# A two-block transformer on one core: the steps of the recurrence, the rotation and the branch products laid out anew

## What is computed

```python
h = rms_norm(x, norm1_g[l])
z = h @ w_in[l]                                  # 1024 -> 8704 columns
zq, zf, zi, zg, zatt, za, zb = split(z)          # q, forget gate, v, output gate, attention, two gates
# recurrence over time, 4 heads of 128, "HgRN2"
log_f = logaddexp(log(lb), log1p(-lb) + log_sigmoid(zf)); k = -expm1(log_f)
S_t = diag(f_t) S_{t-1} + k_t v_t^T;   o_t = S_t^T q_t
o_hg = rms_norm(o_hg, hg_norm_g[l]) * sigmoid(zg)
# attention, 3 groups x 4 heads of 128, windows with dilation 1, 4, 16
qg, kg = partial_rope(qg), partial_rope(kg)      # rotates the first 32 of 128 dims: r1*c - r2*s, r2*c + r1*s
o_att = sum over groups of softmax(lse) * attention(qg, kg, vg)
y = sigmoid(za) * (o_hg @ w_branch_a[l]) + sigmoid(zb) * (o_att @ w_branch_b[l])
x = x + y @ w_out[l]
x = x + square(relu(rms_norm(x, norm2_g[l]) @ w_up[l])) @ w_down[l]
```

## Time and profile before

| | |
|---|---|
| median of 3 runs | 2459.70 us (2459.69 to 2459.79) |
| the profiled execution | 2458.67 us, its span 2457.0 us |
| granted clock of TensorE, mean | 0.955 |
| PE busy | 2200.3 us (90%) |
| DVE busy | 1641.8 us (67%) |
| ACT busy | 1339.4 us (55%) |
| DMA | 506.71 MB, mean 206 GB/s |

### The profile page before, as it was taken

The page is one execution under the profiler, slowest core; times in us unless marked ns, Lnnn a source line. Parts: engine busy times, 40 slices in busy tenths (PEclk is TensorE's granted clock), DMA queues, the critical chain, the costliest instruction groups (busy, mean ns, idle before and its releaser), DMA issues.

```text
span 2457.0 us, 32104 instructions
## 1 busy us (share of the span) xinstructions
PE 2200.3 (90%) x13188; PEld 1936.8 (79%) x13188; DVE 1641.8 (67%) x1980; ACT 1339.4 (55%) x1639; POOL 73.5 (3%) x75
## 2 busy tenths in 40 slices
PE   6789988699999999999995788888998788897998
PEld 6689877588887887878884777887987777796996
DVE  5465564598888988889995686555544577455554
ACT  4534446377777777777773532544543633543543
POOL 2000011000000000000000000000100000000100
PEclk9989989799999999999997899998998999898999
DMA  7345553199999999999993333333554333334552
GB/s 261 103 157 188 189 159 120 58 353 338 347 325 360 334 335 351 326 359 335 341 366 113 120 116 108 120 120 123 187 196 164 125 116 120 103 123 135 166 194 94
DMA packets 379288, 506.71 MB, mean 206 GB/s; under 512 B 11904, under 2 KB 334592, under 8 KB 379136
## 3 DMA queue, kind: packets, MB, share of 16 engines
q1 hardware_dynamic: 374160, 493.92, 60.4%
q10 hardware_dynamic: 4976, 10.68, 1.3%
HBM read 503.51 MB, written 1.05 MB: 205 GB/s over the span
## 4 chain that ended last, share of the span: by engine, by line
PE 75%; DVE 12%; ACT 8%; issue 3%; POOL 1%; DMA 1%; ACTq 0%; DVEq 0%; POOLq 0%
PE bank L360 22%; PE bank L362 22%; PE bank L361 22%; DVE w_low L344 3%; ACT w_high L333 3%; PE bank L1541 1%; PE bank L1129 1%; PE bank L1171 1%; PE bank L1208 1%; DVE hg_att L1702 1%; DVE hg_work L1683 1%; DVE hg_work L1692 1%; DVE hg_work L1690 1%; DVE hg_work L1680 1%; DVE x_low L432 1%
## 5 line engine op out<-in xcount | busy, mean ns | idle before, releaser
L344 DVE TENSOR_TENSOR w_low<-raw,w_high 128x1024 fp32r<-128x1024 f32 x938 | 1131.8, 1228 | 593.5 <-ACT w_high L333 578.0
L333 ACT CAST w_high<-raw 128x1024 fp32r<-128x1024 f32 x938 | 968.2, 1050 | 562.3 <-PE bank L362 555.0
L360 PE MATMUL bank<-x_high,w_high 128*128 128x256 f32 x1888 | 548.8, 291 | 21.6 <-DVE x_low L432 16.6
L362 PE MATMUL bank<-x_high,w_low 128*128 128x256 f32 x1888 | 541.0, 287 | 0.0
L361 PE MATMUL bank<-x_low,w_high 128*128 128x256 f32 x1888 | 539.9, 286 | 0.0
L360 PEld LDWEIGHTS bank<-x_high,w_high 128*128 128x128 f32 x1888 | 365.6, 194 | 43.7 <-issue 37.6
L361 PEld LDWEIGHTS bank<-x_low,w_high 128*128 128x128 f32 x1888 | 366.1, 194 | 0.6 <-issue 0.5
L362 PEld LDWEIGHTS bank<-x_high,w_low 128*128 128x128 f32 x1888 | 363.4, 193 | 0.0
L360 PE MATMUL bank<-w_high,moe_xs_high 128*128 128x512 f32 x704 | 291.5, 414 | 2.0 <-DVE moe_xs_low L1106 1.3
L362 PE MATMUL bank<-w_high,moe_xs_low 128*128 128x512 f32 x704 | 275.9, 392 | 0.0
L361 PE MATMUL bank<-w_low,moe_xs_high 128*128 128x512 f32 x704 | 274.7, 390 | 0.0
(11 more groups left out here) (322 smaller groups left out, 2742.0 us busy)
## 6 DMA issues: line engine op xcount, KB each, us to landing
raw<-in_moe_wg SPq DMA_DIRECT2D x176, 512.0 KB, 5.3
raw<-in_moe_wu SPq DMA_DIRECT2D x176, 512.0 KB, 6.8
raw<-in_moe_wd SPq DMA_DIRECT2D x88, 1024.0 KB, 6.8
raw<-in_w_in SPq DMA_DIRECT2D x84, 1024.0 KB, 5.1
raw<-in_w_up SPq DMA_DIRECT2D x32, 1024.0 KB, 5.5
raw<-in_w_down SPq DMA_DIRECT2D x32, 1024.0 KB, 4.9
raw<-in_w_out SPq DMA_DIRECT2D x16, 1024.0 KB, 4.9
raw<-in_ffn_wg SPq DMA_DIRECT2D x11, 1024.0 KB, 5.3
```

The costliest lines, as they stand in the source:

```text
L333: q.copy(high, raw).then_inc(st.cast, 1)
L344: q.tensor_tensor(low, raw, high.bitcast(F32), ALU.subtract).then_inc(st.low_made, 1)
L360: T.matmul(out, stationary[0], moving[0], start=start, stop=False, skip_group_check=True)
L362: return T.matmul(out, stationary[1], moving[0], start=False, stop=stop, skip_group_check=True)
```

## The change

All of it is in the first half of the two layers of the second block.

- **Steps at fixed pieces.** The recurrence's generators become functions of the slot p. Level li has its subtraction in slot 16+3li, its products on DVE in slot 17+3li, its matmuls in slot 18+3li, its mask in slot 21+3li: three pieces a level. DVE does the step of a slot ahead of its low part, ACT still behind its cast. The second softplus (`scalar_soft`) is in slot 9 instead of 8.
- **Levels on used halves.** DVE subtracts in two operations on the halves of each block (512 columns each) with the sign turned, so that the negative absolute value falls away; the products with k and q are made on 512 columns each.
- **Rotation packed by DMA.** When the six q chunks (then the six k chunks) are evicted, SP issues 12 copies within SBUF that lay the 32 rotated dims of 12 heads on all 128 partitions, once as they are and once with halves swapped; DVE does three operations on 128x768, and 4 copies bring the result back. The twelve matmuls on PE and the 36 operations on DVE go. These DMAs stand in SP's queue between the weight loads, behind waits for the eviction and for the rotation.
- **Attention** begins in slot 53 for heads 0 and 2 and in slot 55 for heads 1 and 3.
- **Branches.** A branch load holds 8 row tiles x 512 columns as two parts, so that a piece is 4 row tiles x 256 columns and ends a bank; its gate product on DVE is one slot behind, and the sums, `x_high` and `x_low` of y follow slot by slot.
- **Evictions and banks.** All evictions are by ACT; the chunks use four banks in turn, and the output gate's chunks come at 18 and 19. `o_hg` and `o_att` now lie in the `att` area, on the former's work and rotation buffers; ACT's `o_hg` waits for the q rotation's copies back.

```diff
-LAYER_COLS = (2, 3, 0, 1, 4, 5, 6, 7) + tuple(range(8, 34))
+LAYER_COLS = (2, 3, 0, 1, 4, 5) + tuple(range(8, 20)) + (6, 7) + tuple(range(20, 34))
...
+def branch_loads(w):
+    w = w.rearrange("(k p) n -> p k n", p=P)
+    return [Load(8, (slice(0, 4), ALL, w[:, :, i * 512:i * 512 + 256]),
+                 (slice(4, 8), ALL, w[:, :, i * 512 + 256:(i + 1) * 512])) for i in range(2)]
...
-ZF, Q, VH, GH, QK, VA, AB = (0, 1), (2, 3), (4, 5), (6, 7), 8, 20, 26
-AT_RECUR, AT_ROPE, AT_ATT = 4, 2 * QK + 2, 2 * AB
+ZF, Q, VH, QK, GH, VA, AB = 0, 2, 4, 6, 18, 20, 26
+AT_BRANCH = 2 * N_COLS
+AT_OUT = AT_BRANCH + 8
+AT_LEVELS = 16
+AT_HG_OUT = AT_LEVELS + 24
+AT_ATT = AT_HG_OUT + 13
+def bank_of(n):
+    return n % 4 if n < AB else n % 2
...
-            ref = blocks[:, :, lv - 1:lv].to_broadcast((P, W4 // (2 * lv), 2 * lv))
-            V.tensor_tensor(a.w0.rearrange("p (n s) -> p n s", s=2 * lv), blocks, ref, ALU.subtract).then_inc(
-                own.sem, 1)
-            V.wait_ge(own.sem, own.up())
-            V.scalar_tensor_tensor(out=a.w0, in0=a.w0, scalar=-1.0, in1=a.w0, op0=ALU.mult, op1=ALU.min).then_inc(
-                k.sem("hg_level"), 1)
+        middle = blocks[:, :, lv - 1:lv].to_broadcast((P, W4 // (2 * lv), lv))
+        V.tensor_tensor(w[:, :, 0:lv], middle, blocks[:, :, 0:lv], ALU.subtract).then_inc(k.sem("hg_level"), 1)
+        V.tensor_tensor(w[:, :, lv:2 * lv], blocks[:, :, lv:2 * lv], middle, ALU.subtract).then_inc(
+            k.sem("hg_level"), 1)
...
-            V.tensor_tensor(a.w1, a.w0, qf, ALU.mult).then_inc(own.sem, 1)
-            V.tensor_tensor(a.w2, a.w0, kf, ALU.mult).then_inc(k.sem("hg_scaled"), 1)
+        V.tensor_tensor(w2[:, :, 0:lv], w0[:, :, 0:lv], kk[:, :, 0:lv], ALU.mult).then_inc(own.sem, 1)
+        V.tensor_tensor(w1[:, :, lv:2 * lv], w0[:, :, lv:2 * lv], q[:, :, lv:2 * lv], ALU.mult).then_inc(
+            k.sem("hg_scaled"), 1)
...
+def sync_rope_in(k, a, layer, which):
+    q.wait_ge(*evicted(k, layer, QK + 6 * which + 5))
+    for row, heads in rope_parts(a, which):
+        q.dma_start(own[row:row + ROPE_DIM, :], heads[0:ROPE_DIM, :]).then_inc(k.sem(f"rope_in{which}"), 16)
+        q.dma_start(swapped[row:row + half, :], heads[half:ROPE_DIM, :]).then_inc(k.sem(f"rope_in{which}"), 16)
+        q.dma_start(swapped[row + half:row + ROPE_DIM, :], heads[0:half, :]).then_inc(k.sem(f"rope_in{which}"), 16)
+def sync_rope_back(k, a, layer, which):
+    q.wait_ge(k.sem("rotated"), 2 * layer + which + 1)
+    for row, heads in rope_parts(a, which):
+        q.dma_start(heads[0:ROPE_DIM, :], a.rope[which][0][row:row + ROPE_DIM, :]).then_inc(k.sem(f"rope_back{which}"), 16)
...
+        V.tensor_tensor(own, own, cos, ALU.mult).then_inc(k.sem("rope_scaled"), 1)
+        V.tensor_tensor(swapped, swapped, sin, ALU.mult).then_inc(k.sem("rope_scaled"), 1)
+        V.tensor_tensor(own, own, swapped, ALU.add).then_inc(k.sem("rotated"), 1)
+ROPE_STEPS = ((AT_HG_OUT, AT_HG_OUT + 1, AT_HG_OUT + 2), (AT_HG_OUT + 4, AT_HG_OUT + 4, AT_HG_OUT + 8))
+def sync_layer(k, a, layer):
+    for which in range(2):
+        sync_weights(k, k.weights, base + 2 * (QK + 6 * which + 6) + 11)
+        sync_rope_in(k, a, layer, which)
+    for which in range(2):
+        sync_weights(k, k.weights, base + ROPE_STEPS[which][2] + 13)
+        sync_rope_back(k, a, layer, which)
...
+        sides.add(AT_ATT + 2 * w, attention(w))
...
+    if u < 2:
+        T.wait_ge(*evicted(k, layer, N_COLS - 2 + u))
+    else:
+        T.wait_ge(k.sem("branch_read"), 8 * layer + u - 1)
```

More of the change, by code:

```diff
@@ L1443 @@
+        with k.area(f"att{layer}") as take:
+            self.gate_ab = take("gate_ab", 16 * S, 16)
+            self.masked = [take(f"masked{w}", 9 * P) for w in range(2)]
+            self.probs_T = [take(f"probs_T{w}", 9 * P) for w in range(2)]
+            self.o_att = [take(n, W4, 4, dt=F32R) for n in ("o_att_high", "o_att_low")]
+            take("gap", 512)
+            self.o_hg = [take(n, W4, 4, dt=F32R) for n in ("o_hg_high", "o_hg_low")]
 class MlpArea:
@@ new lines, with evicted, level_at, tensor_recurrence @@
+ZF, Q, VH, QK, GH, VA, AB = 0, 2, 4, 6, 18, 20, 26
+N_COLS = len(LAYER_COLS)
+AT_BRANCH = 2 * N_COLS
+AT_OUT = AT_BRANCH + 8
+AT_UP = AT_OUT + KT
+AT_LEVELS = 16
+AT_HG_OUT = AT_LEVELS + 24
+AT_ATT = AT_HG_OUT + 13
+def evicted(k, layer, n):
+    return k.sem("evicted"), N_COLS * layer + n + 1
+def bank_of(n):
+    return n % 4 if n < AB else n % 2
+def level_at(p, first):
+    li, rest = divmod(p - first, 3)
+    return li if rest == 0 and 0 <= li < len(HG_LEVELS) else None
+def tensor_recurrence(k, a, layer, p):
+    T, n, levels = k.nc.tensor, layer, len(HG_LEVELS) + 1
+    li = level_at(p, AT_LEVELS + 2)
+    if p == AT_LEVELS:
+        T.wait_ge(k.sem("hg_across"), n + 1)
+        for hh in range(HG_HEADS):
+            mm = T.matmul(k.banks[4][:, hh * P:(hh + 1) * P], as4(a.w1)[:, hh, 0:P], as4(a.w1)[:, hh, P:S],
+                          start=True, stop=True)
+        mm.then_inc(k.sem("hg_across_out"), 1)
+    elif li is not None:
+        T.wait_ge(k.sem("hg_scaled"), len(HG_LEVELS) * n + li + 1)
@@ new lines, in tensor_level, with scalar_soft @@
+def tensor_level(k, a, li, qs, ks):
+    b = 4 + 2 * (li % 2)
+    for hh in range(HG_HEADS):
+        for half in range(2):
+            mm = k.nc.tensor.matmul(k.banks[b + half][:, hh * P:(hh + 1) * P], ks[:, hh, half * P:(half + 1) * P],
+                                    qs[:, hh, half * P:(half + 1) * P], start=True, stop=True)
+    mm.then_inc(k.sem("hg_level_out"), 1)
+def scalar_soft(k, a, src):
+    A_, own = k.nc.scalar, k.own_act
+    A_.activation(a.w0, src, ACT.Abs).then_inc(own.sem, 1)
+    A_.wait_ge(own.sem, own.up())
+    A_.activation(a.w0, a.w0, ACT.Exp, scale=-1.0).then_inc(own.sem, 1)
+    A_.wait_ge(own.sem, own.up())
+    A_.activation(a.w0, a.w0, ACT.Ln, bias=1.0).then_inc(k.sem("hg_soft"), 1)
@@ L1629, in per_head, with vector_recurrence @@
+def vector_recurrence(k, a, layer, p):
+    V, own, n, levels = k.nc.vector, k.own_dve, layer, len(HG_LEVELS) + 1
+    zf, dec4 = flat(a.z_f), as4(a.decay)
     def per_head(cols):
@@ L1882, in vector_attention, with attention_sides, tensor_columns @@
         yield
-def layer_columns(k, layer, n, half):
+def attention_sides(attention):
+    sides = Sides()
+    for w in range(2):
+        sides.add(AT_ATT + 2 * w, attention(w))
+    return sides
+def tensor_columns(k, layer, n, half):
     T = k.nc.tensor
@@ L1890, in layer_columns @@
         T.wait_ge(*x_ready(k, half))
-    before = bank_before(n)
-    if half == 0 and before is not None:
-        T.wait_ge(*chunk_evicted(k, layer, before))
-    product(k, piece, k.x, half, CHUNKS[n][0], n in VH or VA <= n < AB).then_inc(k.used, 1)
-def tensor_layer_first(k, a, layer, src):
-    T = k.nc.tensor
-    sides = Sides()
-    tensor_transposes(k, src, [norm_ready(k, t) for t in range(TT)])
-    sides.add(AT_RECUR, tensor_recurrence(k, a, layer))
-    sides.add(AT_ROPE, tensor_rope(k, a, layer))
-    for n in range(AB):
+    before = n - 4 if n < AB else AB - 2 + n - AB if n < AB + 2 else n - 2
@@ new lines, in tensor_columns, with tensor_branch @@
+    if half == 0 and before >= 0:
+        T.wait_ge(*evicted(k, layer, before))
+    tokens = n in (VH, VH + 1) or VA <= n < AB
+    product(k, piece, k.x, half, bank_of(n), tokens).then_inc(k.used, 1)
+def tensor_branch(k, src, layer, u, ready):
+    T = k.nc.tensor
+    piece = tensor_piece(k, k.weights)
+    for r in ready:
+        T.wait_ge(*r)
+    if u < 2:
+        T.wait_ge(*evicted(k, layer, N_COLS - 2 + u))
+    else:
+        T.wait_ge(k.sem("branch_read"), 8 * layer + u - 1)
+    out = tile2(k.banks[u % 2])
+    for j in range(2):
+        for kk in range(4):
+            mm = three(T, out[:, j, :], [v[:, kk, j * P:(j + 1) * P] for v in piece], [v[:, kk, :] for v in src],
+                       start=(kk == 0 and j == 0), stop=(kk == 3))
+    mm.then_inc(k.used, 1)
```

732 lines of the change are left out of this document (295 added, 437 removed).

## The result

| | |
|---|---|
| median of 4 runs after the change | 2289.38 us (2288.01 to 2292.56) |
| before, on the same chip | 2459.69 us (2456.94 to 2459.79) |
| ratio | 0.9313, 95% interval 0.9301 to 0.9325 |
| profiled execution after | 2292.56 us, its span 2291.2 us, granted clock 0.966 |

The kernel is faster by 170 us. I had predicted 2311 us and a range of 2298 to 2340.

A forecast was written before the change was run, and what follows sets the result against it. PE bounds the kernel, through its holes and low clock. Each first half: 241.5 + 39.6 + 2.3 + 1.5 = 284.9 us, plus 2 allowed; gain 148.7 us, so 2311 us, range 2298 to 2340.

The forecast's parts named there:

- the low-clock part: PE's work at the lower clock in each layer's first half before the change: some 17 us, expected to go.
- Strided halves: DVE's half operations in a level: 0.68 us each; rival of 2.4 us gave 2373 us, chance 0.04.
- The copies over many engines, hidden: Rotation's DMA copies: 2.4 us over 16 engines, no cost taken; rival on one engine 20 us a layer, chance 0.04.
- SP's cover: SP's queue may stand 9 slots, 26 us, less 5.1 us of landing, before weight loads come late.
- the rivals: Stalls stay 2335 us, 0.18; ACT late 2325, 0.05; copies late 2351, 0.04; halves dear 2373, 0.04; slower 0.02; no change 0.01.
- at either price: Levels: PE's 13.8 us of waits go whether a half operation on DVE costs 0.68 or 1.21 us.
- A piece: 2.88 us each: PE's main products in a layer's first half: 76 pieces at 2.88 us, 218.9 us.
- The two allowances of 1 us a layer for thin covers: Possible PE stalls at the layer's head (bounds 0 and 8) and at attention (bounds 0 and 4), 1 us each.
- the rival of ACT's late head: Table loads at the layer's head hold ACT longer, PE stalls: 7 us a layer, 2325 us, chance 0.05.
- the small matmuls: PE's levels, diagonal, full-precision calls, scores and sums of squares in a layer's first half: 39.6 us.
- The hand-offs: PE's changes between the two kinds of matmul: some 20, 1.5 us a half, bounds 0 and 4.
- The first piece: Start of a layer's first half on PE: stays slow, 5.2 us where 2.88 would do, adding 2.3 us.

The follow-up runs named there:

- e4: The changed kernel with level operations on full width (1024 columns) again, in the new order: 2289.95 us.
- e1: The changed kernel with 128 unused bytes in the swap matrix's place, weight buffers at their addresses from before the change: 2301.37 us.
- e8: The changed kernel with ACT's second softplus in slot 8, as before the change: 2289.7 us.
- e16: The changed kernel with attention of both pairs of heads started in slot 53 instead of 53 and 55: 2290.07 us.
- e3: The changed kernel with 256 unused bytes behind its constants: 2289.57 us.
- e13: The changed kernel with 32 unused bytes behind its constants, weight buffers later against the activations, areas keeping their distance from the weights: 2273.47 us.
- e6: The kernel before the change with the rotation left out, q and k entering attention unrotated: 2486.64 us.

## Why the prediction was right, and where it was wrong

**Right.** The forecast was that PE becomes full and stays at the high clock, and so it is, 279.9 of 280.0 us at 0.99. The holes of 48 us a layer, the rotation's matmuls and the low-clock part all went. Strided halves at 0.68 us: 0.69. A period of 10.4 us a level: 10.3. The copies over many engines, hidden: 2.2 us to land. SP's cover: never used up. None of the rivals happened. That the levels' waits would go "at either price" of the half operations holds too, by e4.

**Wrong, first: "A piece: 2.88 us each", taken over from the kernel before.** The row was read rightly, but the price did not belong to the piece. It belonged to the piece with its buffers where they lay, and the diff moved them by 128 B. I read that the swap matrix goes and did not ask what stands behind it in memory. A piece of `w_in` costs 2.84 us after. This is worth 12.0 us by e1's median and takes the result out of the range; at the old place it would have been 2301.4 us. It is 2.3 us a half between halves at the same clock (e1's layer 1 against after), and the rest falls on the other stages, which I had called "as it was". The eight branch pieces are still at 2.88 us, and a piece of `w_out` at 2.81; the 2.83 that I took for it was a mean over two kinds of piece, and came close by luck.

**Wrong, second: the additions.** e1's 2301.4 us is still 9.6 below 2311. The two allowances of 1 us a layer for thin covers made 4 us; measured 0, and e8 and e16 show why. At the head I had put the second softplus's end at 35.3 to 36.6 us, "as it needs a further table load or not". It doesn't: its three functions are absolute value, exp and logarithm, the exp of k stands ahead of it, and only the logarithm has a load before it. It ends 34.9 us behind PE's first product. Timeline of ACT after:

```profile
1353.37 1.28 ACT L1577 ACT_TABLE_LOAD   x1
1354.66 1.06 ACT L1577 ACTIVATE hg_z_f<-hg_work 128x1024 f32<-128x1024 f32 x1
...
1356.57 1.05 ACT L1562 ACTIVATE hg_work<-hg_work 128x1024 f32<-128x1024 f32 x1
1357.65 1.06 ACT L1564 ACTIVATE hg_work<-hg_work 128x1024 f32<-128x1024 f32 x1
1358.73 1.28 ACT L1566 ACT_TABLE_LOAD   x1
1360.03 1.06 ACT L1566 ACTIVATE hg_work<-hg_work 128x1024 f32<-128x1024 f32 x1
```

The rows also answer the rival of ACT's late head: the function starts 0.01 to 0.02 us behind its load, with no drain of 1.38 us beside it. The Trainium skill (ScalarE: Activation LUTs, What ACT_TABLE_LOAD costs) has such a drain; here it isn't seen.

**Wrong, third: the small matmuls,** 39.6 us in the sum and 37.1 measured, 5.0 us over both layers. Levels and diagonal took 13.6 for 14.5, the 140 instructions 14.9 for 15.8, scores 7.3 for 7.5, the sums of squares 1.3 for 1.8. One takes up to 112 ns from start to start; by groups the mean is 100 to 112, since a group's last is followed sooner by a wide product. The hand-offs that I had added, 1.5 us, are about 1.6 in the main products by the same count (242.4 less 68 pieces of 2.84, 8 of 2.88, 8 of 2.81 and the first piece's 2.2). 4 and 5 us are about the 9.6 left; what remains is less than the 2.2 us by which e1's runs differ.

**The first piece** is a term that isn't the kernel's own: 5.0 us at the low clock in both halves of the profiled execution, 2.9 us in one half each of e1 and e3. That is 2.2 us a half by which one execution differs from the next, and a part of the 4.2 us between profiled execution and median.

**The range** was too tight below: its lower end held "6 us for the small sums and pieces taken at their upper prices" and nothing for what moving the buffers could do, which no row of the kernel before shows.

**Still open.** Why the distance acts as it does, in steps and with a period of 256 B, isn't settled, nor why e13 shows two values at one distance. The runs have 16, 32, 64, 128, 224 and 256 B for the weights, and the activations x were never moved, so for products with x their distance to the weights and the weights' own place are not told apart. How the some 158 us of the change at the old place divide among fixed pieces, rotation and branches wasn't taken apart beyond the levels.

## What to carry to other kernels

Before a product's price is taken from a profile, ask whether the change moves its operands: a tensor that goes from the constants shifts all behind it, and one line of padding, swept once, was worth 16 us here. In a stage that waits on a chain of three engines, put the step that others wait for ahead of the routine work in each slot: in the kernel after, going back on that costs 22.6 us and going back on the halves nothing, while in the kernel before the halves alone gave 35 us (the order alone wasn't run there). Work that stands in holes is free and may even keep the clock up, so take the holes away first and the work after.

## What the runs showed of the hardware

- The spacing of PE's matmuls changes with where the operands lie in SBUF: 113.3, 117.3, 118.3 or 120.0 ns for 256 columns in the first block (eight pieces of 24 products: 21.76, 22.53, 22.72, 23.04 us), 227 or 232.6 to 234.3 ns for 512 columns of the experts. 256 B further it is the same (e3). At one place it can still take two values: 113.3 and 117.8 ns in e13.
- The busy time of one product doesn't show it: 280 to 283 ns before and 281 after for 256 columns, though their starts are 120.0 and 118.3 ns apart. The starts of what waits for pieces do.
- Leaving work out slowed the kernel by 26 us (e6): PE had longer holes, and the granted clock was 0.84 instead of 0.98 in the stage of the levels.
- A stretch of products that begins behind a long hole has its first piece at the low clock or not, in kernels alike: 5.0 us after, 2.9 in e1 (layer 0), both behind a wait of 24 us.
- On DVE an operation with blocks down to one column in every two costs what a contiguous one costs, 0.69 us for 512 columns.
